# One block for the shared rotations, the index scores and the differential queries, and three edits at the two ends of the dense experts

## The reference, cut to what matters

```python
def peer_ffn(h, w_query, sub_keys, u_tab, v_tab):
    ...
    def one_block(args):
        h_blk, i_blk, g_blk = args
        u_sel = u_tab[i_blk]
        act = jax.nn.gelu(jnp.einsum('td,thkd->thk', h_blk, u_sel).astype(jnp.float32))
        w = (g_blk * act).astype(h.dtype)
        return jnp.einsum('thk,thkd->td', w, v_tab[i_blk])

def dsa_mixer(q_nope, q_rope, c_kv, k_rope, iq, ik, iw, kv_gain, w_uk, w_uv, pos):
    ...
    c_kv = rmsnorm(c_kv, kv_gain)
    k_rope = rope(k_rope, pos)
    ...
    iq = rope(iq.reshape(B, T, IDX_HEADS, IDX_DIM), pos)
    ik = rope(ik, pos)
    ...
        rel = jax.nn.relu(jnp.einsum('bqhd,bsd->bqhs', qslice(iq, i, Q_BLOCK), ik).astype(jnp.float32) * IDX_DIM ** -0.5)
        score = jnp.einsum('bqhs,bqh->bqs', rel, qslice(iw, i, Q_BLOCK).astype(jnp.float32))
        ...
        _, idx = lax.top_k(score, k_sel)

def diff_mixer(q, k, v, lam, subln_gain, lam_init, pos):
    ...
    q = rope(q.reshape(B, T, B_HEADS * 2, B_QK_DIM), pos).reshape(B, T, B_HEADS, 2, B_QK_DIM)
    k = rope(k.reshape(B, T, B_HEADS * 2, B_QK_DIM), pos).reshape(B, T, B_HEADS, 2, B_QK_DIM)
```

## Time and profile before

| | us |
|---|---|
| median of 3 runs | 3374.61 (3371.51 to 3375.78) |
| the profiled execution, its own time | 3374.93 |
| its span in the profile | 3373.1 |
| TensorE busy | 3227.2 (96%) |
| VectorE busy | 1784.7 (53%) |
| ScalarE busy | 1324.7 (39%) |
| GpSimd busy | 1334.0 (40%) |
| mean granted TensorE clock, share of full speed | 0.971 |

### The profile page before, as it was taken

How to read it: one execution, slowest core, us unless ns; L and a number is a source line. 1 busy time by engine, 2 the same in 40 slices (tenths; PEclk the granted TensorE clock), 3 DMA queues, 4 the chain that set the end, 5 groups by cost and what they waited for, 6 DMA issues and landing times. The chain is left out here.

```text
span 3373.1 us, 48175 instructions
## 1 busy us (share of the span) xinstructions
PE 3227.2 (96%) x16409; PEld 2667.8 (79%) x16414; DVE 1784.7 (53%) x3736; ACT 1324.7 (39%) x2245; POOL 1334.0 (40%) x840
## 2 busy tenths in 40 slices
PE   7999999989989999999999887999999999999999
PEld 6877787879988888888888854578888884578887
DVE  6504333897857777778787457642221236632211
ACT  4233433336653333333333445442322436632222
POOL 2313343359972222222222223434444437644443
PEclk8888999989999999999999988999999999999999
DMA  5221233235669999999998411023333420033332
GB/s 124 77 78 32 56 99 95 69 118 197 211 233 344 329 317 324 325 321 325 322 322 298 103 50 32 26 77 98 99 88 99 122 75 1 4 97 96 97 87 82
DMA packets 453594, 501.90 MB, mean 149 GB/s; under 512 B 77376, under 2 KB 397952, under 8 KB 435536
## 3 DMA queue, kind: packets, MB, share of 16 engines
q1 hardware_dynamic: 429936, 363.12, 35.2%
q0 software_dynamic: 18432, 134.23, 10.8%
q10 hardware_dynamic: 5088, 2.75, 0.3%
HBM read 457.93 MB, written 38.80 MB: 147 GB/s over the span
## 5 line engine op out<-in xcount | busy, mean ns | idle before, releaser
L125 POOL TENSOR_TENSOR w_low<-w_ring,w_high 128x1024 fp32r<-128x1024 f32 (+2 forms) x316 | 752.8, 2386 | 1100.2 <-ACT w_high L120 1070.3
L136 PE MATMUL ps<-h_low,w_high 128*128 128x512 f32 (+1 forms) x2432 | 907.8, 373 | 39.1 <-PEq L631 17.7
L138 PE MATMUL ps<-h_high,w_low 128*128 128x512 f32 (+1 forms) x2432 | 898.9, 370 | 0.0
L137 PE MATMUL ps<-h_high,w_high 128*128 128x512 f32 (+1 forms) x2432 | 898.4, 369 | 0.0
L136 PEld LDWEIGHTS ps<-h_low,w_high 128*128 128x128 f32 x2432 | 462.0, 190 | 106.5 <-POOL w_low L125 19.0
L137 PEld LDWEIGHTS ps<-h_high,w_high 128*128 128x128 f32 x2432 | 461.6, 190 | 58.8 <-issue 1.2
L138 PEld LDWEIGHTS ps<-h_high,w_low 128*128 128x128 f32 x2432 | 461.0, 190 | 56.1
L120 ACT ACTIVATE w_high<-w_ring 128x1024 fp32r<-128x1024 f32 (+3 forms) x318 | 323.6, 1022 | 136.4 <-PE ps L138 115.2
L136 PE MATMUL ps<-v_low,top 128*128 128x512 f32 x768 | 300.4, 391 | 4.9 <-DVE v_low L125 4.9
L138 PE MATMUL ps<-v_high,top_at 128*128 128x512 f32 x768 | 301.7, 393 | 0.0
L137 PE MATMUL ps<-v_high,top 128*128 128x512 f32 x768 | 301.5, 393 | 0.0
(11 more groups left out here) (546 smaller groups left out, 5415.6 us busy)
## 6 DMA issues: line engine op xcount, KB each, us to landing
w_ring<-in_peer_uv_dram SPq DMA_DIRECT2D x128, 512.0 KB, 5.7
u_raw<-in_peer_uT_dram SPq DMA_DIRECT2D x78, 512.0 KB, 5.7
w_ring<-in_peer_uT_dram SPq DMA_DIRECT2D x50, 512.0 KB, 3.7
w_ring<-in_ffn_w_gate_dram SPq DMA_DIRECT2D x44, 512.0 KB, 3.7
w_ring<-in_ffn_w_up_dram SPq DMA_DIRECT2D x44, 512.0 KB, 3.7
w_ring<-in_w_in_dram SPq DMA_DIRECT2D x36, 512.0 KB, 3.7
w_ring<-in_ffn_w_down_dram SPq DMA_DIRECT2D x32, 448.0 KB, 3.6
peer_gates<-room SPq DMA_DIRECT2D x6, 2048.0 KB, 7.4
```

The lines of the kernel that those rows point to most:

```text
L125: return eng.tensor_tensor(rounded(low), whole, high, ALU.subtract)
L136: nc.tensor.matmul(out, rounded(w_high), rounded(x_low), start=start, stop=False, **more)
L137: nc.tensor.matmul(out, rounded(w_high), rounded(x_high), start=False, stop=False, **more)
L138: return nc.tensor.matmul(out, rounded(w_low), rounded(x_high), start=False, stop=stop, **more)
```

## The change

`project_both` becomes `project_in_turn` for any number of programs. The body of `project_rope` becomes `rotation`, which returns its programs, and the shared rotations, the index scores and the queries run in one block. The four transposes of the latents move from behind the rotations to behind the second tile of their second turn, into bank 6, and their copy to behind ScalarE's work on the first tile of that turn. TensorE's first four index steps wait each for the bank of one tile of the rotations. The queries get a tail of 16 spinning matmuls.

In `peer_gates` ScalarE copies the first experts' gates of the twelfth block from `spread` to SBUF at the end of its program. In `peer_experts` SyncE's wait for the last store goes from chunk 0 to the gates' load of chunk 4, so that the loads of chunks 2, 3 and 4's u stand ahead of it; and TensorE ends with 12 spinning matmuls.

```diff
@@ projection @@
-        act.wait_ge(bank_free, per_turn * (turns + 1))
+        if not followed:
+            act.wait_ge(bank_free, per_turn * (turns + 1))
...
+    def tile_free(pe, b):
+        pe.wait_ge(bank_free, freed(turns, b))
@@ rotation @@
             split(b)
+            if inside and ("act", i, b) in inside:
+                inside["act", i, b](eng)
...
     def pe(eng, i, b, bank_free):
+        if inside and ("pe", i, b) in inside:
+            inside["pe", i, b](eng, lambda tiles: eng.wait_ge(bank_free, per_turn + tiles))
@@ peer_gates, scalar @@
                 for q in range(quads - GROUP, quads):
                     copy(DENSE - 1, q)
+                act.wait_ge(copied, DENSE * quads)
+                nc.scalar.activation(opening.gates[:, BLOCKS - 1, :], spread[(BLOCKS - 1) % 2][:, 0:QUAD, :].rearrange("p i t -> p (i t)"), ACT.Copy).then_inc(last_gates, 1)
+                act.wait_ge(last_gates, 1)
@@ peer_experts, sync @@
-                    if b % QUAD == 0:
+                    if b % QUAD == 0 and not (first and b == 0):
                         hold(sp, gated, r * PER + (b + QUAD), c.sp_tick)
-                        if first and b == 0:
+                        if first and b == QUAD:
                             sp.wait_ge(route.stored[1], 16 * (BLOCKS // 2))
-                            opening.load_gates(sp, route, BLOCKS - 1, BLOCKS)
-                        else:
-                            gates_of(r, b)
+                        gates_of(r, b)
@@ peer_experts, tensor @@
                 turns(pe, step)
+                pe.wait_ge(gelued, 2 + TURNS * FULL)
+                spin(c, 6, 12)
@@ peer_experts, vector @@
-                    dve.wait_ge(gates_in[quad], r * (8 * (PER // QUAD)) + 16 * (b // QUAD // 2 + 1) + (16 if quad == 0 else 0))
+                    dve.wait_ge(gates_in[quad], r * (8 * (PER // QUAD)) + 16 * (b // QUAD // 2 + 1))
@@ even_mix @@
-                project_rope(c, w["shared"], lambda i, b: angles[4 * i + b], lambda i, b: scales[4 * i + b], lambda i, b: dests[4 * i + b], w["qk"],
-                             latents_before, latents_after, unturned=len(dests), dims=[64 if of is tables[64] else 32 for of in angles])
-            search = differential(c, w, tables[64], vb, oT, lam, score, best, left, add_mask, lambda ctx: index_scores(c, ctx, iqT, ikT, iw, score, best, left, up, oT[:, 4:8, :]))
+                shared = rotation(c, rotating, w["shared"], lambda i, b: angles[4 * i + b], lambda i, b: scales[4 * i + b], lambda i, b: dests[4 * i + b], w["qk"],
+                                  latents_before, unturned=len(dests), dims=[64 if of is tables[64] else 32 for of in angles], inside=inside, followed=True)
+                indexed = index_scores(c, rotating, iqT, ikT, iw, score, best, left, up, oT[:, 4:8, :], shared)
+                search = differential(c, w, tables[64], vb, oT, lam, score, best, left, add_mask, qkT, rotating, shared, indexed)
@@ differential @@
+    queries = rotation(c, rotating, w["qk"], [rope64] * 4, lambda i, b: lam.of_turn[:, i:i + 1] if isinstance(i, int) else lam.of_turn[:, bass.ds(i, 1)],
+                       lambda i, b: tile_of(qkT, i, 4, b), w["nope"], {"dve": lead}, beside=beside_queries, behind=indexed, tail=(0, 16))
+    project_in_turn(c, shared, indexed, queries)
+    rotating.__exit__()
@@ latents @@
-    def turn(pe):
+    def turn(pe, tiles_free):
         pe.wait_ge(normed, TT)
-        pe.wait_ge(banks_read, 1)
+        tiles_free(3)
         for t in range(TT):
-            tr = nc.tensor.transpose(c.ps[:, 0, t * P:(t + 1) * P], ckv[:, t, :], c.ident[:, :])
+            tr = nc.tensor.transpose(c.ps[:, 6, t * P:(t + 1) * P], ckv[:, t, :], c.ident[:, :])
         tr.then_inc(turned, 1)
...
-    return {"sp": sp_part, "act_first": act_first, "act": act_part, "dve": dve_part}, {"pe": turn, "act": copy}
+    return {"sp": sp_part, "act_first": act_first, "act": act_part, "dve": dve_part}, {("pe", 1, 0): turn, ("act", 1, 0): copy}
@@ index_scores @@
-            if n >= 4:
+            if n < 4:
+                shared.tile_free(pe, n)
+            else:
                 pe.wait_ge(rectified, n - 3)
```

More of the change, by code:

```diff
@@ L911, in project_swiglu, with project_rope, rotation @@
                       after={"dve": lambda eng: eng.wait_ge(dest_low, 2 * w.turns + 2)}), ready
-def project_rope(c, w, tables, scales, dest, ahead=None, before={}, after={}, beside=None, unturned=None, first=None, dims=None):
+def project_rope(c, w, tables, scales, dest, ahead=None, before={}, after={}, beside=None, unturned=None):
+    with c.stage() as ctx:
+        project_in_turn(c, rotation(c, ctx, w, tables, scales, dest, ahead, before, after, beside, unturned))
+def rotation(c, ctx, w, tables, scales, dest, ahead=None, before={}, after={}, beside=None, unturned=None, dims=None, inside={}, **more):
@@ new lines, in rotation @@
+    moved = None if dims is None else ctx.sbuf("moved", [P, per_turn, T])
+    copied, swapped, scaled = ctx.sem("copied"), ctx.sem("swapped"), ctx.sem("scaled")
+    table = tables if callable(tables) else lambda i, b: tables[b]
+    turned = lambda i, b: unturned is None or i * per_turn + b < unturned
+    by_pe = lambda i, b: dims is not None and dims[i * per_turn + b] != 64
+    swaps_before = lambda i, b: sum(by_pe(0, x) for x in range(i * per_turn + b)) if dims is not None else 0
+    quarters = [(slice(32 * q, 32 * q + 32), slice(32 * (q ^ 1), 32 * (q ^ 1) + 32)) for q in range(4)]
@@ L970 @@
+    return projection(c, ctx, w, {"act": act, "pe": pe, "dve": dve}, ahead=ahead, before=before, after=after,
+                      unrolled=("all" if unturned is not None else () if beside is None else ("dve",)), **more)
 ROWS_N = 256
@@ new lines, in differential, with beside, head @@
+    project_in_turn(c, shared, indexed, queries)
+    rotating.__exit__()
+    rest = [(n, tiles) for n in range(beside_tiles + 1, beside_tiles + 5)]
+    def beside(dve, s):
+        if 1 <= s <= len(rest):
+            take_best(c, Chain(dve, c.dve_step), score, best, left, rest[s - 1][1], rest[s - 1][0])
+    def head(s):
+        half = lambda m: slice(64 * m, 64 * m + 64)
+        return dict(scores=lambda m: [(qkT[half(m), s, :], qkT[half(m), s + DIFF_H, :])], mask=None, v=lambda m, j: vb[:, j, s * P:(s + 1) * P],
+                    mix=lam.minus[:, 0:1], out=lambda m: c.ps[:, 7, :], first=True, last=True, sink=oT[:, s + 4, :])
@@ L3726, in nothing @@
         pass
[L3728 removed]
+    return Programs(nothing, nothing, tensor, scalar, vector, shared.slots_free, None)
 def take_best(c, step, score, best, left, tiles, n):
```

152 lines of the change are left out of this document (62 added, 90 removed).

## The result

| | before | after |
|---|---|---|
| median of 5 runs, us | 3375.78 (3371.51 to 3377.07) | 3353.06 (3348.94 to 3361.30) |
| profiled execution, us | 3374.93 | 3360.9 |
| its span, us | 3373.1 | 3359.1 |
| mean granted TensorE clock | 0.971 | 0.974 |

The ratio is 0.9949, with a 95% interval of 0.9932 to 0.9965: 17.2 us less, between 11.8 and 23. The change makes the kernel faster by more than the 0.2% that can be told from no change. The forecast was 17.6 us and a time of 3357.0. That the total fits so well is partly luck: one of its four terms was 3.7 us too large, and the other three together 3.0 us too small.

The account below looks back on a forecast made before the run. TensorE, busy for 96% of the span, was taken to bound the kernel. Gains of 10.7 + 1.2 + 4.5 + 1.2 = 17.6 us from 3374.93 gave 3357.3, so 3357.0 for the median; range 3352 to 3364.

Parts of the forecast that it names:

- Part 1: Opening of the experts: loads and gates no longer wait for the last store; gain 10.7 us, from 7.3 to 11.7.
- the u tile's landing: Opening of the experts: chunk 3's u tile, issued near 1002, lands at 1009.5; bounds 1008 and 1012.9.
- the bound for sharing: Opening of the experts: u tile lands at 1012.9 if its loads share evenly with the store and gathers push in.
- Tight, but enough: Opening of the experts: loads from 1005 to 1033 are some 9.4 MB; 28 us at 340 GB/s would hold 9.5.
- the two signs of being wrong: Experts: the u tile lands behind 1013, or new waits on a DMA appear in the loop.
- the rule that the prediction took from the Trainium skill: DMA landing: a semaphore step lands only after every earlier write of that DMA engine, so the store is reported first.
- Part 2: Experts' end: twelve spinning matmuls stay hidden and may keep the transposes at full clock; gain 1.2 us, from -0.5 to 2.5.
- Part 3: Seam between rotations and index scores: barriers removed, transposes cost 0.5; net gain 4.5 us, from 2.0 to 5.5.
- Part 4: Queries' end: one barrier less gives 0.4, the clock kept up by spinning 0.8; gain 1.2 us, from 0.2 to 2.2.
- The late u tile: Opening of the experts: u tile lands at 1016 or later, queue shared with gathers; sum 11, 3364 us; chance 0.13.
- The slower case: Experts' loop falls behind its loads once every turn, 4.1 us a stop, 29 in 7 turns; 3386 us; chance 0.04.
- The spins without effect: Experts' end and queries' end: the clock falls anyway despite spinning matmuls; 2.0 us less gain, 3359; inside the range.

Follow-up runs that it names:

- the last variant: Changed kernel with chunk 3's u tile issued behind the early hidden values but ahead of chunk 2's v, and the keys' transposes earlier: 3356.83 us, ratio 0.9957.
- the hand-over alone: Changed kernel, but SyncE waits for the last store at chunk 0 again; the twelfth block's gates still come by ScalarE's copy: 3366.34 us, ratio 0.9990.
- the one with both edits: Changed kernel with chunk 3's u tile issued first, the keys' transposes earlier and 10 spinning matmuls behind them: 3358.95 us, ratio 0.9961.

## Why the prediction was right, and where it was not

**Part 1 was mis-sized: 10.7 forecast, 7.0 measured, 0.3 below its lower bound.** The mechanism was right. VectorE waits for the memset, chunk 0 starts 6.1 us behind it (6.4 in the sum), the gathers go out at 1003.51 and 1005.50, 6.6 and 8.6 behind it (6.5 and 8.5), and nothing in the turns behind the opening waits for them. The failed step is the u tile's landing. It was put at 8.4 us behind the memset and came at 10.4 to 10.7. Of these 2.1 to 2.4 us, 0.8 are the issue (1.6 to 1.8 us behind the memset, not 0.9), and 1.3 the way from issue to split, 8.6 to 8.9 us instead of 7.5. I had read the end of the store's data from a trace in which the queue ran empty behind it, and counted only what was ahead of the tile. In the changed kernel two more loads are issued within 2 us behind it, and no slice of the 36 us is under 255 GB/s. The same reading had the store's data end at 1005; the slices of the earlier trace rows show small rates until 1006.5, so the landing came 0.8 us behind the last data and not more than 2. And the prediction's count of all loads, 9.4 MB in 28 us, was low: from 3.9 to 31.9 us behind the memset the changed kernel moved 10.9 MB, at 390 GB/s. The measured landing stands nearer to the bound for sharing (1012.9, which is 11.8 behind the memset) than to the value taken.

From there TensorE idles 2.90 us instead of 0.5, and works at 0.83 of the clock for 10 us, which is 1.7 more. Together 4.1. The two variants that met the same split with a gap of 1.0 to 1.1 us and no low clock behind it had chunk 1's product 1.4 to 1.8 us earlier, which bears out the price of the clock. In return the 0.5 us that I had charged for chunks 1 and 2 don't appear, and chunk 1 starts 3.4 to 3.7 us later than forecast. The loop itself keeps the gain: it takes 848.5 to 848.9 us from chunk 1's product to the transposes, against 848.5 and 849.5 before. So the claim that every us of the opening is kept to the end held for the change, but the variants show how near the edge it was: 3 to 4 us more of opening gave back 0.8 to 4.8 in the loop. "Tight, but enough" was right by about that margin. Of the two signs of being wrong, the landing stayed under its limit (10.7, where 1013 is 11.9 behind the memset). The other, a new wait on a DMA in the loop, did appear once, ScalarE's 3.80 us at 1026.48, but TensorE had no gap from it.

On landing, the rule that the prediction took from the Trainium skill (DMA: Bandwidth & Descriptors, "Queues, rings and completion order") stays consistent with the rows: with the u tile issued first its split starts 1.0 us behind GpSimd's release by the store (7.8 and 6.8 behind the memset), never ahead of it. No run here tells that rule from plain order. The same section says that each DMA engine goes round between the queues it has work for; that the gathers, on another queue, lengthen the later tile's way (14.5 us from issue to split in the last variant, 11.3 in the changed kernel) would fit it, but no run took the gathers away.

**Part 2 was right:** 1.8 against 1.2, inside its bounds. The clock held through the transposes (3.68 us), the additions moved up with them, and the spinning matmuls were hidden but for about 0.1 us (last product to transposes 4.65 us, 4.55 before; 4.75 and 5.09 in the later profiles, 4.95 in the second of before). The kernels without them put the price of leaving them out at 1.0 to 1.9 in this stretch.

**Part 3 was right in its terms:** the transposes cost 0.49 (0.5), the sixth score comes 4.8 us earlier relative to the rotation (5.2), 4.3 net. The other 1.0 of the 5.3 was not forecast. It lies between the sixth score and the queries, where the granted clock was 0.83 and is 1.00 in the same steps. Windows of the 15 us ahead of the queries and the 10 behind, kernel before:

```profile
1994.50:2009.50 15.00, 10.43 (x24) 3.84 (x23) 14.27 (x40) 9.72 (x20) 0.00 (x0) 0.83 0.00 1
2009.50:2019.50 10.00, 9.97 (x33) 8.04 (x34) 8.93 (x20) 2.17 (x5) 2.75 (x1) 0.74 0.20 52
```

and the changed kernel, third profile:

```profile
1977.60:1992.60 15.00, 10.43 (x33) 4.01 (x31) 14.26 (x39) 10.09 (x20) 0.00 (x0) 1.00 0.00 1
1992.60:2002.60 10.00, 10.00 (x44) 8.32 (x45) 9.62 (x23) 3.67 (x6) 3.33 (x2) 1.00 0.20 52
```

**Part 4 was right for another reason.** One barrier less gives 0.5 (7.22 to 6.70 us without the spin; 0.4 forecast). The tail was to give 0.8 and gives nothing net. The larger part is the second row of each fence: in the ten us behind the queries' start the clock rose from 0.74 to between 0.83 and 1.00. That is 0.9 to 2.6 us which the sum did not have.

So part 1 was 3.7 too large, and parts 2 to 4 were too small by 0.6, 0.8 and 1.6, most of it clock around the queries that was in no term. The total stood 0.7 from the forecast.

**The rivals.** The late u tile (landing at 1016 or later) did not come, but half of its reason did, the shared queue. Its 3364 rested on part 1 giving 4. The slower case did not occur in the changed kernel. It was seen once each in two variants, at 4.5 and 4.8 us, near the 4.1 that the prediction priced for one stop. It came once and not in every turn: behind the opening no wait of TensorE on a load's split appears, and in the last variant the queue was busy 0.91 of the time from 1040 to 1860, where it had been full until 1030. The spins without effect were half true.

## What to carry to other kernels

When loads are moved ahead of a wait and the queue was idle there, count the whole traffic of the next 30 us against its full rate, and take the landing from that count too, not just from the bytes ahead of the tile that is needed first. The rate that filled the hole is also the new limit, and two of the three reorderings here only chose which tile was late. An edit that lets a consumer start earlier and leaves its loads where they were can cost time (the hand-over alone: 4 us in its one profile). And where gaps of 2 to 4 us lie on a path with a clock gate, read several profiles by stretches before a us or two is put down to an edit.

## What the runs showed of the hardware

**The same idle stretch can leave the clock up or take it down.** At the queries' end TensorE idles 2.10 us in all three profiles of the changed kernel, and then does the same 8 matmuls. First, second and third profile, one fence each:

```profile
2043.85 2.52 PE L131 MATMUL ps<-mask_causal,mask_ident 128*128 128x512 bf16 x8 [2.10 <-PEq L205]
```
```profile
2036.75 1.89 PE L131 MATMUL ps<-mask_causal,mask_ident 128*128 128x512 bf16 x8 [2.10 <-PEq L205]
```
```profile
2041.93 3.57 PE L131 MATMUL ps<-mask_causal,mask_ident 128*128 128x512 bf16 x8 [2.10 <-PEq L205]
```

1.89 us is full clock (2.4 GHz), 3.57 half (1.2 GHz), 2.52 a change in between. The same holds ahead of the rotations, in untouched code: behind an idle stretch of 2.24 to 2.33 us the next ten us ran at a granted clock of 1.00 in both profiles of before, in the run with only the opening, and in the one with both edits, and at 0.83 in nine others. In the five variants with the same 2.10 us the 8 matmuls took 1.89 us three times, 2.44 and 2.65. The profile with 3.57 is the only one of the eight in which the queries' first ten us ran at 1.00 (0.72 to 0.83 in the others); whether the two belong together was not tried. So a spin that shortens an idle stretch buys a chance, not a duration.

**A load's issue can hold its engine.** Behind six or seven loads issued within 7 us, SyncE's next issue, chunk 4's v, took 6.4 and 6.6 us in the kernel before, 8.2 to 8.9 in the changed one and up to 10.4 in the variants (10.08 above), where most others take 0.3 to 0.9. Everything later on SyncE stood behind it. The prediction counted the waits of SyncE's order, but not that an issue itself can be held. What sets the length was not tried.
